# Sparse attention's compression in a two-block model: the tap layout and the position vector's products

## What is computed

```python
def compress_kv(kv, pe, w1, w2):        # kv: (b, 512, 4 groups, 64)
    b, s, g, d = kv.shape
    n_str = s // CMP_STRIDE             # CMP_STRIDE = 16, CMP_LEN = 32
    per = CMP_LEN // CMP_STRIDE
    n_cmp = n_str - per + 1             # 31
    c = kv.reshape(b, n_str, CMP_STRIDE, g, d)
    blocks = jnp.concatenate([c[:, j:j + n_cmp] for j in range(per)], axis=2)
    blocks = blocks + pe[None, None, :, None, :].astype(kv.dtype)
    flat = jnp.transpose(blocks, (0, 1, 3, 2, 4)).reshape(b, n_cmp, g, CMP_LEN * d)
    return jax.nn.silu(flat @ w1) @ w2
```

## Time and profile before

| | |
|---|---|
| Device time, median of 3 runs | 3609.72 us (3604.08 to 3613.27) |
| Span of the profiled execution, first to last instruction | 3607.4 us |
| Busy: PE / PEld / DVE / ACT / POOL | 96% / 75% / 55% / 20% / 2% |
| Chain that ended last: PE / DVE / rest | 88% / 8% / 4% |
| Mean granted clock of TensorE | 0.978 |
| The step in question, with its neighbours | 1014 to 1062 us of the span |

### The profile page before, as it was taken

How to read it: one execution, slowest core, us unless ns; L and a number is a source line. 1 busy time by engine, 2 the same in 40 slices (tenths; PEclk the granted TensorE clock), 3 DMA queues, 4 the chain that set the end, 5 groups by cost and what they waited for, 6 DMA issues and landing times.

```text
span 3607.4 us, 43951 instructions
## 1 busy us (share of the span) xinstructions
PE 3446.0 (96%) x16699; PEld 2722.7 (75%) x16699; DVE 1998.2 (55%) x4671; ACT 715.4 (20%) x1763; POOL 88.1 (2%) x105
## 2 busy tenths in 40 slices
PE   8987999999999999999998988999999999999988
PEld 3484788888754568888887766888887888887766
DVE  4472367554404784675544558643354656558566
ACT  2231021100013551211001135022212011121143
POOL 0000000000000000000000021000000000000110
PEclk9998999999999999999999999999999999999999
DMA  3200312222210003122222220212211222102311
GB/s 130 82 13 27 125 47 82 94 82 94 105 47 36 16 33 118 58 82 82 94 82 82 71 83 24 82 71 77 74 65 45 102 74 89 41 24 84 112 42 48
DMA packets 39975, 254.09 MB, mean 70 GB/s; under 512 B 5796, under 2 KB 5924, under 8 KB 11616
## 3 DMA queue, kind: packets, MB, share of 16 engines
q1 hardware_dynamic: 31616, 224.41, 17.6%
q0 software_dynamic: 3664, 15.07, 1.2%
q10 hardware_dynamic: 4496, 11.89, 1.2%
HBM read 242.68 MB, written 2.18 MB: 68 GB/s over the span
## 4 chain that ended last, share of the span: by engine, by line
PE 88%; DVE 8%; issue 2%; ACT 1%; DMA 1%; ACTq 0%; POOL 0%; POOLq 0%; DVEq 0%
PE PL L1212 26%; PE PX L1212 20%; PE PL L923 14%; PE PL L1560 4%; PE PL L1407 3%; PE PL L907 2%; PE PX L1669 2%; DVE SCR L2972 2%; PE PL L1325 1%; DVE SCR L2987 1%; PE PL L1585 1%; PE PX L1345 1%; PE PL L1712 1%; PE PL L1374 1%; PE PX L933 1%
## 5 line engine op out<-in xcount | busy, mean ns | idle before, releaser
L923 PE MATMUL PL<-xn,ring 128*128 128x264 f32 (+1 forms) x1600 | 501.6, 471 | 11.2 <-DVE xn L2366 10.7
L923 PEld LDWEIGHTS PL<-xn,ring 128*128 128x128 f32 x1600 | 304.4, 192 | 193.7 <-issue 161.8
L2409 DVE TENSOR_TENSOR Z<-PL,SCR 128x512 f32<-128x512 f32 (+3 forms) x104 | 63.9, 614 | 447.0 <-PE PL L923 349.2
L1212 PE MATMUL PL<-Z,ring 128*128 128x256 f32 (+1 forms) x1248 | 297.4, 389 | 10.4 <-DVE Z L3362 8.6
L1212 PEld LDWEIGHTS PL<-Z,ring 128*128 128x128 f32 x1248 | 241.3, 194 | 49.8 <-DVE Z L3362 9.7
L1212 PE MATMUL PL<-AUX,ring 128*128 128x256 f32 (+1 forms) x1056 | 243.9, 379 | 0.0
L1212 PEld LDWEIGHTS PL<-AUX,ring 128*128 128x128 f32 x1056 | 200.6, 190 | 27.6 <-DVE AUX L2740 0.2
L1212 PE MATMUL PL<-xn,ring 128*128 128x264 f32 (+1 forms) x864 | 204.2, 389 | 12.7 <-DVE xn L2366 11.6
L1212 PEld LDWEIGHTS PL<-xn,ring 128*128 128x128 f32 x864 | 165.8, 192 | 42.9 <-issue 12.1
L1840 ACT ACTIVATE SCR<-PL 128x256 f32<-128x256 f32 (+1 forms) x72 | 27.6, 383 | 737.2 <-PE PL L1212 737.2
L1212 PE MATMUL PX<-Z,AUX 128*128 128x264 f32 (+1 forms) x704 | 163.8, 384 | 2.7 <-DVE Z L3170 2.7
(11 more groups left out here) (514 smaller groups left out, 6043.3 us busy)
## 6 DMA issues: line engine op xcount, KB each, us to landing
ring<-w_tiles SPq DMA_DIRECT2D x212, 1024.0 KB, 4.8
Z<-Z ACTq DMA_DIRECT2D x16, 264.0 KB, 5.0
SCR<-head_rows POOLq DMA_DIRECT2D x16, 264.0 KB, 3.7
AUX<-norm_scratch POOLq DMA_DIRECT2D x8, 528.0 KB, 6.6
cst<-consts ACTq DMA_DIRECT2D x1, 2188.5 KB, 15.4
resid<-x ACTq DMA_DIRECT2D x4, 512.0 KB, 9.3
Z<-norm_scratch POOLq DMA_DIRECT2D x4, 512.0 KB, 8.0
AUX<-mem POOLq DMA_DIRECT2D x2, 1024.0 KB, 5.1
```

Of the source, the lines that this page charges most:

```text
L923: mm = pe.matmul(PL[:, 2 * h + c, 0:e - a], ring[t % 2][:, k, P * h:P * h + P], src_block(name, k)[:, a:e], start=k == 0, stop=k == KB - 1)
L1212: mm = pe.matmul(ps, lhs(k), rhs(k), start=kc == 0 and k == 0, stop=kc == per - 1 and k == 3)
L2409: ins = dve.tensor_tensor(d, ps, f, ALU.mult)
```

## The change

1. The tile `two` becomes `taps`, of the same size and in the same place. For each pair of taps l it holds the 31 columns of each group side by side, so that the moving operand of product l is four runs of 32 consecutive elements.
2. ScalarE's four copies of 512 (or 511) columns per block become eight of 8 x 31 columns each: two per half of the partitions and group, the second (`late`) starting 16 tokens later. They read every 16th token and write runs of 31.
3. The position vector becomes a 32nd column of each group, written by one more ScalarE copy of 4 x 16 elements for keys and one for values (in blocks b = 0 and b = 2).
4. The 16 single-column products are gone. The 16 others have 128 columns instead of 124, and `pecol` is read from column 31.

```diff
-        two = AUX[:, 4096:8192].rearrange("p (x g t) -> p x g t", x=2, g=4)
+        taps = AUX[:, 4096:8192].rearrange("p (x g l n) -> p x g l n", x=2, g=4, l=16)
@@ compressed(x), TensorE
-                    hp = ps[:, 0:124].rearrange("p (g n) -> p g n", g=4)
+                    hp = ps[:, 0:P].rearrange("p (g n) -> p g n", g=4)
                     for l in range(16):
-                        pe.matmul(hp, w1[:, x, l, :], two[:, x, :, 2 * l:2 * l + 16 * (NCMP - 1) + 1:16],
-                                  start=l == 0, stop=l == 15)
-                    for l in range(16):
-                        mm = pe.matmul(ps[:, 124:125], w1[:, x, l, :], Q("pe", 16 * x + l, 16 * x + l + 1),
-                                       start=l == 0, stop=l == 15)
+                        mm = pe.matmul(hp, w1[:, x, l, :], taps[:, x, :, l, :], start=l == 0, stop=l == 15)
                     mm.then_inc(t_ps, 1)
@@ nsa(ready), ScalarE
-                    act.activation(two[0:64, x, g, :], Z1[0:64, 8 + b, :], ACT.Copy)
-                    act.activation(two[64:128, x, g, 0:T1 - 1], ps[64:128, 1:T1], ACT.Copy)
-                    act.activation(two[0:64, x, g + 1, :], ps[0:64, :], ACT.Copy)
-                    act.activation(two[64:128, x, g + 1, 0:T1 - 1], Z1[64:128, 8 + b, 1:T1], ACT.Copy).then_inc(t_sb, 1)
+                    if g == 0:
+                        biases = Q("pe", 16 * x, 16 * x + 16).rearrange("p (a l) -> p a l", a=1).broadcast_to([P, 4, 16])
+                        act.activation(taps[:, x, :, :, NCMP], biases, ACT.Copy)
+                    for r, k, y in ((0, 0, Z1[:, 8 + b, :]), (1, 0, ps), (0, 1, ps), (1, 1, Z1[:, 8 + b, :])):
+                        rows = slice(64 * r, 64 * r + 64)
+                        for late in range(2):
+                            tokens = y[rows, 16 * late:16 * (late + NCMP)]
+                            tokens = tokens.rearrange("p (n l r) -> p r l n", l=8, r=2)[:, r]
+                            ins = act.activation(taps[rows, x, g + k, 8 * late:8 * late + 8, 0:NCMP], tokens, ACT.Copy)
+                    ins.then_inc(t_sb, 1)
@@
-                    step(act.activation(pecol[:, x:x + 1], ps[:, 124:125], ACT.Copy))
-                    hp = ps[:, 0:124].rearrange("p (g n) -> p g n", g=4)
+                    step(act.activation(pecol[:, x:x + 1], ps[:, NCMP:NCMP + 1], ACT.Copy))
+                    hp = ps[:, 0:P].rearrange("p (g n) -> p g n", g=4)[:, :, 0:NCMP]
```

## The result

The changed kernel takes 3591.33 us (median of 5 runs, 3588.0 to 3595.45), the kernel before 3609.72. The ratio of the two is 0.9949 with a 95% interval of 0.9939 to 0.996, so 14 to 22 us less; the forecast was 3589.5, in a range of 3583 to 3599. Timed again beside two of the experiments, the changed kernel came out at 3588.29 us, ratio 0.9939 (0.9926 to 0.9953).

What follows compares the result with a forecast made beforehand. PE, busy for 96% of the span, was taken as the bound. Terms 10.45 + 3.33 + 6.46 = 20.2 us off the 3607.4 us span give 3587.2, plus 2.3 to the median: 3589.5 us, range 3583 to 3599.

Steps and rivals of the forecast that it cites:

- Part 1: Compression step on PE: dropping the single-column products takes 5.20 + 5.25 = 10.45 us off the chain.
- Part 2: Units 7 and 8, behind the single-column products: TensorE's clock stays up, each takes 6.87 us, gaining 3.33 us.
- Part 3: Compression products on consecutive columns: 32 pieces take 3.56 us instead of 6.79, twice, gaining 6.46 us.
- The first rival: Compression products keep their 212 ns pace despite the new layout; gain only 13.8 us, 3595.9 us; chance 0.11.
- Part 4: ScalarE's new strided copies ahead of the compression: longer blocks, but covered by 3.7 us of slack, so no cost.
- the bounds: ScalarE's copies per block: 3.1 us without a stride penalty, 4.8 us with time per element doubled; both cost nothing.
- Part 5: Behind the compression: Silu, next weight tile and evacuation stay off the chain; later streams only start earlier, no cost.
- a clock that falls anyway: Rival at the compression: 128-column products also lower TensorE's clock; some 15 us gain, 3595; 0.05 jointly with falls later.
- more falls later: Rival behind the step, from the attention on: two or three extra clock falls leave 15 to 17 us; joint chance 0.05.
- the point where all blocks queue up: Rival at ScalarE's copies: above 0.96 us each they queue, from 1.55 us the gain is gone; slower kernel 0.02.

Runs made afterwards that it cites:

- Experiment 2: The kernel before without its single-column products, strided layout kept, position vector left out; 3598.80 us, ratio 0.9965.
- experiment 3: The kernel before with 64 columns instead of one in the position vector's products, same instructions and weight loads; 3602.47 us, ratio 0.9976.
- Experiment 1: The kernel before with only the side-by-side layout of the taps, single-column products with the position vector kept; 3602.03 us, ratio 0.998.
- experiments 4 to 6: The changed kernel with taps interleaved so the moving operand steps 2, 4 or 16 elements; executed once each: 3584.15, 3601.93 and 3591.02 us.
- experiment 8: The changed kernel with four half-swap products cut to one column, ScalarE copying across partition halves instead; 3588.09 us, ratio 0.9941, and again 3590.20 us.

## Why the prediction was right

- *Part 1, the single-column products.* 10.45 us, as its rows said. Experiment 2 has it together with part 2: 13.8 us on the chain, as worked out.
- *Part 2, the clock.* 3.33 us, and both units take 6.87 in the changed kernel. That it is the emptiness of the products which costs the clock is shown by experiment 3, with the same instructions and more columns. Experiment 1 corrects a detail: where the fall comes isn't fixed, and what it costs went from 1.8 to 3.5 us there.
- *Part 3, the layout.* Forecast 3.56 us for the 32 pieces, measured 3.57, twice. The stride was only argued, by exclusion; experiments 4 to 6 show it. The first rival (no change of pace, 13.8 us in all) is out.
- *Part 4, ScalarE.* Forecast at no cost, and at no cost it stayed. The duration lay between the bounds, since one half of the copies met each of them. The SBUF reads took 610 ns, where a doubling of the time per element gives 616, and the PSUM reads 366, where no penalty gives 370. What the Trainium skill says of lines of 16 bytes ("SBUF — State Buffer", section "Door 1: The DMA port swizzle") it says of SBUF, and the SBUF reads agree with it. I had put that penalty on the PSUM reads too in the upper bound, and with this stride they cost nothing. A block took 3.57 us, between 3.1 and 4.8.
- *Part 5, behind the step.* The next weight tile came in time (PE's chain has no gap up to 1070 us). The attention took 185.7 to 185.8 us in both kernels, and nothing was given back there or behind it. That was luck in good part: the prediction gave 0.05 to a clock that falls anyway or to more falls later, and six of the nine other kernels lost 1.5 to 6 us in this way (experiment 8). It also called fewer falls as likely as more, and no execution shows an attention shorter than that of the kernel before. What decides it is open.
- *The total.* The 20.2 us on the chain are 18.4 us between the medians, which is inside the scatter: the runs of the changed kernel alone spread over 7.5 us.

## What to carry to other kernels

Price a moving operand by its step before its columns: at 16 bytes and more the 128 columns of float32 here took twice as long, and an idle engine that lays the data side by side gets that back as long as it ends before the product needs it. A product with one column isn't cheap. Each such piece cost about as much as one with 64 or 128 columns (108, 110 and 112 ns at full clock) and, in a run of 32, the clock of the next unit too, so a column like this belongs into a product that is done anyway. And work out by how much the helper may be late before it costs: the slack in one block, and the point where all blocks queue up, came out of two subtractions here, 1.55 us a copy where 1.52 made the kernels level. Add to it what the clock costs after the wait. Last, a gain of a few us ahead of a long stretch of short products isn't safe before the time of that stretch has been read too.

## What the runs showed of the hardware that I had not expected

- ScalarE's stride penalty depends on where it reads: a step of 64 bytes cost 200 ns for 248 elements from SBUF, and nothing from PSUM. A strided write to SBUF cost 235 ns (366 to 601), and a strided read and a strided write together took 620, so they didn't add up.
- TensorE's moving operand took 227 ns a piece with a step of 16 bytes and 218 with one of 64, both twice the 112 of consecutive elements, and 113 with a step of 8 bytes.
- ScalarE moved 64 partitions to the other 64 in a copy at no extra time (32 copies, half of them moving: 602 to 632 ns, median 614, against 610 in the changed kernel).
- A gain of 2.6 us ahead of the attention was followed by 3.1 us more at the lower clock within it, and 3 us more behind it, the same in two executions of that kernel, while the predicted kernel showed none in two. In all profiled executions the attention's length took one of three values, 185.8, 187.2 or 188.9 us, give or take 0.1.
